# One load queue, two buffers of their own: the first conformer units prepared during the feed-forward, and attention overlapped with its neighbours

## What is computed

```python
for layer in range(2):
    if layer % 2 == 0:
        h = rms_norm(x, even_norm_g[i])
        x = x + even_mixer(h, ...)        # forgetting attention (8 heads of 64) and multiscale pooling
    else:
        h = rms_norm(x, odd_norm_g[i])
        x = x + conformer_conv(h, ...)    # pw1 -> a * sigmoid(g) -> 31 causal taps -> LN -> silu -> pw2
    h = rms_norm(x, ffn_norm_g[layer])
    x = x + conv_ffn(h, ...)              # up (1024 x 5632) -> 3 taps -> silu(gate) * val -> down (2816 x 1024)
```

## Time and profile before

| | |
|---|---|
| median of 3 runs | 1711.32 us (1709.49 to 1712.39) |
| profiled execution | 1717.11 us, span 1715.3 us |
| TensorE busy | 1691.2 us |
| VectorE busy | 1094.5 us |
| ScalarE busy | 692.3 us |
| GpSimd busy | 152.7 us |

### The profile page before, as it was taken

The page is one execution under the profiler, slowest core; times in us unless marked ns, Lnnn a source line. Parts: engine busy times, 40 slices in busy tenths (PEclk is TensorE's granted clock), DMA queues, the critical chain, the costliest instruction groups (busy, mean ns, idle before and its releaser), DMA issues.

```text
span 1715.3 us, 21745 instructions
## 1 busy us (share of the span) xinstructions
PE 1691.2 (99%) x7795; PEld 1383.4 (81%) x7795; DVE 1094.5 (64%) x1676; ACT 692.3 (40%) x992; POOL 152.7 (9%) x146
## 2 busy tenths in 40 slices
PE   8999999999999999999999999999999999999999
PEld 7888878888888789788888888887656888888888
DVE  6799884343534686555663663679997666366364
ACT  4322362222223345544432432447665443243242
POOL 1000400000000050000000000005881000000000
PEclk9999999999999999899999999999999999999999
DMA  8776314233333134603232322223211322223222
GB/s 277 224 242 220 126 49 128 93 98 98 117 98 98 49 99 111 161 25 99 98 98 98 98 98 87 79 80 99 74 49 41 108 98 98 92 92 110 75 84 87
DMA packets 186259, 182.56 MB, mean 106 GB/s; under 512 B 4136, under 2 KB 182572, under 8 KB 186188
## 3 DMA queue, kind: packets, MB, share of 16 engines
q1 hardware_dynamic: 186188, 181.62, 33.6%
HBM read 173.15 MB, written 2.10 MB: 102 GB/s over the span
## 4 chain that ended last, share of the span: by engine, by line
PE 89%; DVE 4%; ACT 2%; issue 2%; POOL 1%; SPq 1%; DMA 0%; DVEq 0%; POOLq 0%; ACTq 0%
PE PSUM L1801 23%; PE PSUM L1803 23%; PE PSUM L1802 23%; PE PSUM L2346 1%; POOL CP L604 1%; PE PSUM L2387 1%; PE PSUM L2388 1%; PE PSUM L2389 1%; SPq L472 1%; PE PSUM L2184 1%; PE PSUM L2185 1%; PE PSUM L2186 1%; DVE PSUM L1733 1%; PE PSUM L2159 1%; PE PSUM L1833 1%
## 5 line engine op out<-in xcount | busy, mean ns | idle before, releaser
L644 ACT ACTIVATE WH<-RAW 128x1024 fp32r<-128x1024 f32 x274 | 281.7, 1052 | 717.3 <-PE PSUM L1803 677.0
L1801 PE MATMUL PSUM<-XH,WH 128*128 128x512 f32 x1152 | 449.5, 390 | 0.0
L1803 PE MATMUL PSUM<-XH,WL 128*128 128x512 f32 x1152 | 448.2, 389 | 0.0
L1802 PE MATMUL PSUM<-XL,WH 128*128 128x512 f32 x1152 | 448.2, 389 | 0.0
L1105 DVE TENSOR_TENSOR WL<-RAW,WH 128x1024 fp32r<-128x1024 f32 x274 | 336.1, 1249 | 7.9 <-ACT WH L644 7.8
L1802 PEld LDWEIGHTS PSUM<-XL,WH 128*128 128x128 f32 x1152 | 216.2, 188 | 45.6 <-issue 0.7
L1801 PEld LDWEIGHTS PSUM<-XH,WH 128*128 128x128 f32 x1152 | 216.2, 188 | 45.6 <-issue 0.7
L1803 PEld LDWEIGHTS PSUM<-XH,WL 128*128 128x128 f32 x1152 | 216.2, 188 | 44.8
L1801 PE MATMUL PSUM<-HH,WH 128*128 128x512 f32 x620 | 241.9, 390 | 0.4
L1803 PE MATMUL PSUM<-HH,WL 128*128 128x512 f32 x620 | 241.2, 389 | 0.0
L1802 PE MATMUL PSUM<-HL,WH 128*128 128x512 f32 x620 | 241.2, 389 | 0.0
(11 more groups left out here) (381 smaller groups left out, 2081.7 us busy)
## 6 DMA issues: line engine op xcount, KB each, us to landing
RAW<-in_ffn_w_up SPq DMA_DIRECT2D x44, 1024.0 KB, 5.1
ARAW<-in_ada_w SPq DMA_DIRECT2D x24, 1024.0 KB, 5.2
RAW<-in_mlp_w_in SPq DMA_DIRECT2D x16, 1024.0 KB, 5.3
RAW<-in_mlp_w_out SPq DMA_DIRECT2D x16, 1024.0 KB, 5.1
RAW<-in_ffn_w_down SPq DMA_DIRECT2D x16, 1024.0 KB, 5.2
RAW<-in_sc_w_in SPq DMA_DIRECT2D x9, 1024.0 KB, 5.1
RAW<-in_even_w_in SPq DMA_DIRECT2D x8, 1024.0 KB, 5.6
RAW<-in_odd_w_pw SPq DMA_DIRECT2D x16, 512.0 KB, 5.4
```

The costliest lines, as they stand in the source:

```text
L644: act.activation(WH[:, j, a:b, :], RAW[:, j, a:b, :], ACT.Copy).then_inc(s_hi, 1)
L1801: pe.matmul(o, wh, mh[:, k, :], start=(k == 0), stop=False)
L1802: pe.matmul(o, wh, ml[:, k, :], start=False, stop=False)
L1803: mm = pe.matmul(o, wl, mh[:, k, :], start=False, stop=(k == kn - 1))
```

## The change

There are two sets of edits.

**Attention.** The scores of steps 0 and 1 are multiplied within the last v unit, before its last block; VectorE's copies of that unit's first two blocks wait for these blocks alone (`h_mm`). ScalarE's two V copies move from before the steps into step 2. The constants of slots 2 and 3 are copied from those of slots 0 and 1 by two more DMAs each in heads 2 and 3, and GpSimd's two memsets and the wait on them go. The load of U_EOUT + 2 moves from behind head 3 to behind head 5. The pooled half of U_EOUT + 1 is multiplied piece by piece within the last four steps.

**The first two conformer units.** They are loaded into a buffer RAWX and split into WHX and WLX, which take room that attention and the output projection have left. ScalarE and VectorE do this behind the down units of groups 0 and 1. The first pair of loads stands ahead of feed-forward 0's loads and waits for `s_mm` of U_EOUT + 4, the second stands behind group 1's up loads. The ordinary units 2 and 3 of the conformer are loaded and split where units 0 and 1 were. Down unit U_PW1 - 2 is multiplied whole, with waits for each half of its weight, so that only U_PW1 - 1 is taken by halves; six small copies on VectorE bring the counters of the skipped units up to date. One filling matmul is put before the last channel sums of the conformer.

```diff
+        RAWX = at("RAWX", 172.625, [P, 8, UW])
+        WHX = [at("WHX_0", 128, [P, 8, UW], F32R), at("WHX_1", 148.5, [P, 8, UW], F32R)]
+        WLX = [at("WLX_0", 136, [P, 8, UW], F32R), at("WLX_1", 156.5, [P, 8, UW], F32R)]
...
                 if h == 2:
                     sp.wait_ge(s_mm, U_EVEN + 8)
-                    sp.wait_ge(s_zero, 6)
...
+                if 2 <= h < SLOTS:
+                    for dst, src in ((QR[1][DH + 2:DH + 4, place, :], QR[0][DH + 2:DH + 4, place, :]),
+                                     (KR[1][DH:DH + 2, place, :], KR[0][DH:DH + 2, place, :])):
+                        sp.dma_start(dst.bitcast(F32), src.bitcast(F32)).then_inc(s_hd[slot], 16)
...
-            load(U_EOUT + 2, 0, eout, 2 * UW)
             load_head(4)
             load_head(5)
+            load(U_EOUT + 2, 0, eout, 2 * UW)
             load_head(6)
...
+            def first_conf_unit(n):
+
+                if n == 0:
+                    sp.wait_ge(s_mm, U_EOUT + 4)
+                else:
+                    sp.wait_ge(s_fl, 3)
+                for h in range(2):
+                    sp.dma_start(RAWX[:, :, h * P:h * P + P], pw1[:, :, h, n * P:n * P + P]).then_inc(s_fw, 16)
+
             def feed_forward(layer):
                 up, down = wview("ffn_w_up_2", layer), wview("ffn_w_down_2", layer)
                 u = U_FFN[layer]
+                if layer == 0:
+                    first_conf_unit(0)
                 for first, steps, kn in GROUPS:
                     with sp.Fori(0, steps) as it:
                         load(it * 2 + u, 0, up, it * UW + first * UW)
                         load(it * 2 + (u + 1), 1, up, it * UW + (F2 + first * UW))
+                    if layer == 0 and first == 4:
+                        first_conf_unit(1)
...
-            for n in range(DC):
+            for n in range(2, DC):
                 sp.wait_ge(s_lo, halves(U_PW1 + n - 2, 2))
...
+                        if layer == 0:
+                            n = first // 4
+                            act.wait_ge(s_fw, 48 + 32 * n)
+                            for k in (slice(0, 4), slice(4, 8)):
+                                act.activation(WHX[n][:, k, :], RAWX[:, k, :], ACT.Copy).then_inc(s_fh, 1)
...
+                        if layer == 0:
+                            n = first // 4
+                            for half, k in enumerate((slice(0, 4), slice(4, 8))):
+                                dve.wait_ge(s_fh, 2 * n + half + 2)
+                                tt(WLX[n][:, k, :], RAWX[:, k, :], WHX[n][:, k, :].bitcast(F32), ALU.subtract
+                                   ).then_inc(s_fl, 1)
...
-                if n < DC - 1:
+                if n == 0:
+                    lo_half(U_PW1 + 3, 1, 0)
+                    lo_half(U_PW1 + 3, 1, 1)
+                elif 2 <= n < DC - 1:
                     lo_half(U_PW1 + n + 2, j, 0)
                     lo_half(U_PW1 + n + 2, j, 1)
...
+                    if j == 1 and b == 2:
+                        mm.then_inc(h_mm, 1)
+                    if j == 1 and b == 3:
+                        pe.wait_ge(e_ln, 8)
+                        pe.wait_ge(s_ev, U_EVEN + 7)
+                        scores(0)
+                        scores(1)
...
+                if s >= 4 * HEADS - 1:
+                    nth = s - 4 * HEADS + 1
+                    if nth == 2:
+                        pe.wait_ge(a_e, 4 * HEADS - 2)
+                    for n in (nth % 2 * 2, nth % 2 * 2 + 1):
+                        out_part(U_EOUT + 1, n, 1 - nth // 2)
...
-                        half_product(u + 2, 0, h + 2 * first, kn)
+                        product(u + 2, 0, HH, HL, kn, s_h, h + 2 * first)
                         half_product(u + 3, 0, h + 2 * first, kn)
-                        half_product(u + 2, 1, h + 2 * first, kn, (0,))
+                        half_product(u + 3, 1, h + 2 * first, kn, (0,))
                         pe.wait_ge(s_r, ST_X3)
                         half_sum(0)
-                        half_product(u + 2, 1, h + 2 * first, kn, (1,))
-                        half_product(u + 3, 1, h + 2 * first, kn)
+                        half_product(u + 3, 1, h + 2 * first, kn, (1,))
...
+                if n == DC - 1:
+                    pe.wait_ge(s_ev, U_PW2 - 1)
+                    keep_busy(1, 0)
...
-                            wh, wl = (w[:, 0, k, c * P:c * P + P] for w in (WH, WL))
+                            wh, wl = (w[:, k, c * P:c * P + P] for w in (WHX[0], WLX[0]))
```

More of the change, by code:

```diff
@@ L733, in split_half_pair, with early_hi @@
                                    ).then_inc(sp_h, 1)
+            def early_hi(n, half):
+                u, j = U_PW1 + n, n % 2
+                act.wait_ge(s_mm, u - 3)
+                act.wait_ge(s_raw[j], u * 8 - (16, 8)[j])
+                act.wait_ge(s_gate[j], (n - j) * 8 + 16)
+                a, b = (0, 4) if half == 0 else (4, 8)
+                act.activation(WH[:, j, a:b, :], RAW[:, j, a:b, :], ACT.Copy).then_inc(s_hi, 1)
             def split_unscaled(stat, c, gain, k):
@@ L899, in _ @@
             for s in range(4 * HEADS + 2):
+                if s == 2:
+                    act.wait_ge(s_rc, 1)
+                    act.wait_ge(s_mm, U_EVEN + 8)
+                    last_v_rows(2)
+                    last_v_rows(3)
                 if s >= 2:
@@ L1532, in _ @@
                 u, j = U_EVEN + p, p % 2
[L1533 removed]
+                if p == 7:
+                    dve.wait_ge(h_mm, 1)
+                else:
+                    dve.wait_ge(s_mm, u + 1)
                 if p < 2:
@@ L2102, in head_sums, with scores @@
                     pe.matmul(PS_[:, 6 + n % 2, :], BDR[:, :], SQL[:, n % 2, :], start=False, stop=True).then_inc(s_hn, 1)
+            def scores(s):
+                h, qb, n = s // 4, s % 4, (s % 4 + 1) * P
+                slot, place = h % SLOTS // 2, h % 2
+                q = slice(qb * P, qb * P + P)
+                pe.wait_ge(s_hd[h % SLOTS], 16 * (OPERANDS * (h // SLOTS + 1) + (2 if slot else 0)))
+                if s == 2:
+                    pe.wait_ge(s_ev, U_EVEN + 8)
+                if s >= 3:
+                    pe.wait_ge(a_e, s - 2)
+                bank = PS_[:, S_BANKS[s % 3], :]
+                pe.matmul(bank[:, 0:n], QHL[slot][:, place, q], KHH[slot][:, place, 0:n], start=True, stop=False)
+                pe.matmul(bank[:, 0:n], QR[slot][:, place, q], KR[slot][:, place, 0:n], start=False, stop=True)
+                pe.matmul(bank[:, n - P:n], IDENT[:, :], MASK[:, :], start=False, stop=True,
+                          skip_group_check=True).then_inc(a_s, 1)
             for p in range(2, 6):
@@ L2188, in out_chunk @@
                     mm.then_inc(s_mm, 1)
-            for n in range(4):
-                out_chunk(U_EOUT, n)
+            out_chunk(U_EOUT, 0)
             pe.wait_ge(a_oe, 32)
@@ L2196, in _ @@
                                  ).then_inc(a_ot, 1)
-            for n in range(4):
-                out_chunk(U_EOUT + 1, n)
+            for n in range(1, 4):
+                out_chunk(U_EOUT, n)
             for u in (U_EOUT, U_EOUT + 1):
@@ L2253, in half_product @@
                     pe.wait_ge(s_ev, u - 1)
-                    pe.wait_ge(s_lo, halves(u, 2))
                 for c in parts:
                     for k in range(kn):
+                        if half == 0 and c == 0:
+                            if k in (0, 4):
+                                pe.wait_ge(s_lo, halves(u, k // 4 + 1))
+                            pe.wait_ge(s_h, base_ + k + 1)
                         wh, wl = (w[:, j, k, c * P:c * P + P] for w in (WH, WL))
@@ L2366, in first_unit_by_halves @@
                             mm = pe.matmul(o, wl, XH[:, k, tokens(half)], start=False, stop=(k == 7))
-                        if half == 0 and k == 3:
+                        if half == 0 and k == 1:
                             half_sum(1)
@@ L2375, in unit_with_taps @@
                 for k in range(8):
-                    if k == 0 or k == 4:
+                    if n == 1 and k == 0:
+                        pe.wait_ge(s_fl, 5)
+                    if n > 1 and k % 4 == 0:
                         pe.wait_ge(s_lo, halves(u, k // 4 + 1))
```

147 lines of the change are left out of this document (63 added, 84 removed).

## The result

The changed kernel takes **1722.24 us** (median of 6 runs, 1720.14 to 1730.66), the kernel before 1711.61 (6 runs, 1709.49 to 1715.05). The ratio is 1.0067, 95% interval [1.0049, 1.0084], so 8.4 to 14.4 us slower. The forecast was 1715.2 with a range up to 1721.5: the sign came, the size didn't.

The account below looks back on a forecast made before the run. TensorE, busy nearly throughout, was taken as the bound, with VectorE setting the conformer's pace. Terms 13.5 - 5.2 - 0.5 - 0.9 - 2.3 - 0.7 = +3.9 on 1711.3 gave 1715.2 us, range 1708.5 to 1721.5.

Parts of the forecast that it names:

- The base: Sum made against the profiled execution, 1717.11 us; the plain runs' median is 5.8 us lower, a difference carried over unchanged.
- part 2: Attention: moved output load ends head 4's wait and low clock, 5.2 us gained; output products in last steps, 0.5 more.
- part 5: Layer norm after the conformer: filling matmul holds the clock for the last sums, 0.7 us gained (0 to 1.3).
- rival A: Attention gains only 2.3 us: a new wait drops the clock, or plain runs never had it low; 1718.1, chance 0.20.
- Part 1: Load queue before the first feed-forward: new wait stalls TensorE 11.65 us, then 1.8 at low clock; loss 13.5 (12.6 to 17.1).
- Rival C: Not slower: at the stall both megabytes land after 6.8 us, loss 11.4 us, total 1713.1; chance 0.22.
- Rival B: After the new stall the clock stays low for 10 us, costing 4.2 or 5 instead of 1.8; 1718, chance 0.08.
- Part 3: End of first feed-forward: TensorE's low-half waits go, shorter cover adds new ones; 0.9 us gained (0.3 to 1.3).
- Part 4: Conformer: VectorE's WL work of 2.36 us after window 1 is gone; 2.3 us gained (1.0 to 2.5).
- rival D: No stall at all, since loads behind the new wait are not late: -9.6, 1701.7; chance 0.08 including the unforeseen.

Follow-up runs that it names:

- experiment 14: Kernel before with only both 1 MB output loads moved behind head 7; 1709.35 us, ratio 0.9990.
- experiment 9: The changed kernel run again with no edit, for a second profile; 1721.23 us, ratio 1.0057.
- experiment 4: Kernel before with the attention edits alone; 1713.20 us, ratio 1.0010.
- experiment 3: Changed kernel with the first pair of RAWX loads issued behind group 0's up loads; 1707.79 us, ratio 0.9977.
- experiment 5: Conformer edits and filling matmul on the attention of the kernel before, first RAWX pair behind group 0's up loads; 1706.81 us, ratio 0.9973.
- experiment 11: Experiment 7 with slots 2 and 3's constants copied once for both heads, and the first RAWX pair back ahead of the feed-forward loads; 1717.43 us, ratio 1.0031.
- experiment 7: Experiment 3 with both 1 MB output loads issued behind head 7; 1704.74 us, ratio 0.9965.
- experiment 10: Changed kernel with 22 filling matmuls before the first feed-forward product; 1729.49 us, ratio 1.0107.
- experiment 12: Experiment 5 with both 1 MB output loads issued behind head 7; 1704.76 us, ratio 0.9961.
- experiment 6: Kernel before with only the filling matmul ahead of the last channel sums; 1710.19 us, ratio 0.9996.
- experiment 2: Kernel before with only the wait for the four output units ahead of the feed-forward loads, no added load; 1721.97 us, ratio 1.0063.
- experiment 1: Kernel before run again with no edit, to read each run's mean clock; 1710.40 us, ratio 0.9994.

## Why the prediction was wrong, point by point

**The base: wrong, and the cause of the miss.** "The median of the plain runs is 5.8 us lower; I carry the difference over unchanged." That difference was clock: 4.8 us at head 4 (10.62 against 5.80 at full clock) and 1.5 at the layer norm, in one execution, slower than all of the 93 plain runs. The gains that I then took from just these two places (4.2 of part 2, 0.7 of part 5) were gains against an execution that the median doesn't resemble. This was the second half of rival A, with a chance of 0.20 and a price of 2.9 us. The price was too small: it left part 2 its wait and part 5 its clock. The measured time is 7.0 us above the forecast, and the attention's 5.7 are most of that.

**Part 2, attention: -5.7 forecast, about 0 found.** "So that one late operand costs 2.6 + 4.2 = 6.8 us": experiment 14 takes it away and finds 1.7 (0.2 to 3.3). And the change put four waits in its place, so that at full clock the stage is as long as before (113.47 against 113.32). The arithmetic of their places was good: head 3 waits, as forecast, and heads 6 and 7 wait behind the moved megabyte. Its sizes were low: in the first profile two steps of head 6's copies took 1.3 and 2.0 us where such steps mostly take 0.6 and 1.2, and TensorE went at 725.4, not 722.6 (0.9 of that lies ahead of attention, in code that didn't change). The forecast of "no operand wait over 1.5 us" failed with 1.52 and 1.89, and that of no window at 0.50 in attention held in the first profile and failed in the second (experiment 9). In experiments 4 and 9 the clock fell behind such a wait; in experiment 9 that cost nothing. In the medians attention is worth +1.0 (experiment 3 against 5) to +2.2 (experiment 4); the interval of experiment 4 includes 0, and those of 3 and 5 overlap.

**Part 1, the new wait: right, slightly low.** Forecast 11.65 idle and 1.8 of clock; found 11.56, 11.69, 11.96 and 1.5 to 2.4. Landing after the wake: 8.9 forecast, 9.1 found. Rival C, with 6.8 us for both megabytes, is refuted by that row. The Trainium skill ("DMA: Bandwidth & Descriptors", section "Anatomy of one DMA") gives its formula as a fit for single DMAs issued by GpSimd. The prediction carried it over to loads issued by SyncE, and there the trace doesn't agree with it: 9.1 us. The 14.0 of experiment 11 is within the bounds of 12.6 to 17.1. Rival B didn't come: some 3, 5 and 4 us of low clock after work resumed (the two profiles of the changed kernel and experiment 11), not 10.

**Part 3: right, a bit better than thought.** 0.9 forecast (0.3 to 1.3); the feed-forward stage without the stall's clock is 389.20 in experiment 3 against 390.7, 1.5, just above the range. The wait on XL at unit 0 is 0.75 us, as forecast (0.7), the second one between the halves is not there.

**Part 4: right.** 2.3 forecast, 2.4 found (116.22 to 113.81), and 113.8 to 113.9 in experiments 3, 5, 7, 9, 10, 11 and 12.

**Part 5: right mechanism, wrong base.** All profiles with the filling matmul have the clock at 1.00 there and 7.1 us for the stage, but so do two of the five without it (experiment 6). The median gains 0.7 by a measurement that can't tell it from nothing.

**The corrected sum**: 14.0 for the wait, 0 for attention (-1 to +2), -1.5, -2.4, and for the last sums -0.5, an estimate between nothing and the 0.7 of experiment 6: +9.6. Measured: +10.6 and, in the ninth experiment, +10.3. The three gains together, 4.4, are what experiment 5 measures alone: 4.0 by the medians, 4.6 by the ratio. And rival D's number, the change without its stall, was 1701.7; experiment 3 gave 1707.8. The 6 us between are again the base and attention.

## What to carry to other kernels

A load queue in program order makes one wait a wait for everything behind it: put a load whose buffer comes free late behind the loads that are wanted soon, and keep megabytes out of a chain of small copies on which TensorE lives. Before a gain is taken from a low clock or a single late operand in one profile, ask whether the plain runs have it: a profile some microseconds above their median has something that they mostly lack, and a change can't take away what isn't there. Idle stretches that stay can be filled, for the clock's sake, once one filling matmul has been timed.

## What the runs showed of the hardware

The clock's answer to the same idle stretch varies from run to run. After 2.6, 2.85, 2.13 and 2.38 us of waiting at head 4 it was at 0.50 for about 10, 7, 3 and 0 us (before, experiments 2, 1 and 5). After 2.03 to 2.05 us before the last sums it fell in three profiles (before, 1 and 2) and stayed in two (4 and 14). Waits of 1.47 and 1.77 us were followed by 0.50 as well (experiments 9 and 4), while the first profile of the changed kernel had 1.89, the tenth experiment's 1.95, and both kept 1.00. The Trainium skill ("TensorE: Matmul & The Clock Gate", section "The HAM clock gate") says of the slow stretch at a kernel's start that its length differs between runs of one kernel. These rows show the same for stretches in the middle of one, and add that whether one comes at all differs too.

Small copies issued by SyncE mostly take 0.6 us each to issue, but single ones take 1.3 to 2.3. Most profiles have one near 698 to 700 us and one near 714 to 717 (699.39 in experiment 3; 699.59, 714.81 and 716.80 in the changed kernel), some have them elsewhere, and experiment 7's has none. A head's eight copies, 5.2 us, then miss TensorE's pace of 5.8 to 6.2 us a head. What makes them slow isn't shown.
